# Between norm and feed-forward products: ScalarE writes the full normalised values, VectorE two low halves, three convolutions use two PSUM banks each

## The chip, the cores and the metric

The kernel runs on one core of a Trainium2 chip. The metric is the device time of one execution in microseconds, as the median of several runs. A core has TensorE (matrix products, in the profile PE, with its weight loads PEld), VectorE (DVE), ScalarE (ACT), GpSimd (POOL) and SyncE (SP, here the queue of most DMAs). Matrix products write PSUM, which has eight banks of 512 float32 columns in each of 128 partitions; GpSimd works on SBUF alone.

## What is computed

One layer of a hybrid trunk for 1024 latent tokens and 128 context tokens that share weights: a normalisation, a mixer (a gated convolution group and a gated DeltaNet group), an output projection, and then the part that matters here:

```
h  = rmsnorm(x, norm2_w) * (1 + scale2) + shift2
u, gt = split(h @ w_up)            # 2816 features each, 22 blocks of 128
gt = grid_conv3x3(gt, ffn_conv_w)  # depthwise; the context is one row
x  = x + gate2 * ((gelu(gt) * u) @ w_down)
```

Everything is float32. The kernel holds a matrix operand as a high half (rounded to the type that TensorE reads fast) and a low half (the remainder), and forms a product as high x high, low x high and high x low, three matmuls for each pair of tiles.

## The kernel before

Features lie on the partitions (8 tiles k of 128 make 1024), tokens along the columns: T = 1152, of which 1024 latent and 128 context. The five engines run programs of their own, each in the order written, and meet by semaphores; nothing is scheduled by a planner. `LATE` only gives old semaphores new names; `after(engine, what, n)` waits for one of those.

**Second norm (11 parts, list `NORM2`).** Parts 0 to 2 are the first 768 columns of tiles 0 to 2, parts 3 to 7 all columns of tiles 3 to 7, parts 8 to 10 the last 384 columns of tiles 0 to 2. For each part VectorE writes the scaled values (`scaled`, L2581) into one of two buffers `ub2`; ScalarE adds the shift and writes the high half `hH` (`high_part`, L1822); VectorE writes the low half `hL` (`low_part`, L2591); GpSimd adds both halves and writes the full value over X (`h_part`, L1607), once the old X is saved in DRAM (`x_out`). A 128-column and a 1024-column (or 256-column) instruction make up a part where latent and context differ. TensorE multiplies each part as it comes with the weights of two blocks (`norm2_step`, L3163): gate block 0 and gate block 1. Then come two more plain blocks, U_FFN+2 (the up half of block 0) and U_FFN+3 (gate block 2), 72 matmuls of 384 columns each. ScalarE copies gate block 0 into the padded grid G (`evac_rows`, L1856), gate blocks 1 and 2 into `fa` (`stage_gate`, L2056).

**Steps of seven products.** The remaining up and gate blocks are made two at a time, in 20 steps m, by a seven-product scheme (order P1, P5, P6, P3, P7, P2, P4; `FORMS`). A product is 24 matmuls of 288 columns. It needs sums of quarters of the input, made from the full values: VectorE writes four sums T1s, T3s, T2s, T4s (L2639 to L2644, 128x2304 each), ScalarE their high halves (`input_high`, L2095), GpSimd their low halves (`input_low`, L1621). It also needs sums of the weights (GpSimd, `sum_1` to `sum_4`), and of each the high half (ScalarE, `form_high`, L2090) and the low half (GpSimd, `form_low`, L1627). In a step, ScalarE copies P1, P5 and P6 out of PSUM (`copy_out`, L2114), and VectorE adds the later products: `c12` after P3, `c22_sum` after P7, `c11` after P2 (L2697, L2717), `c21` after P4 (L2725); GpSimd does `c22`. TensorE's P2 waits for `c12`, its P4 for `c22_sum`, the next step's P1 and P5 for `c11` and `c21`.

**Convolutions.** `conv9(f)` on VectorE makes block f of 22: nine taps over G on 1024 latent columns (L2664, L2667) and three on 128 context columns (L2665, L2669). The accumulator of f = 0 is the SBUF tile `fa[:, 0]`; from f = 1 it is four PSUM banks (2 to 5), 256 columns in each. The steps' combinations are written into it by hand: `beside={5: (c12, 0)}` puts `c12(0)` behind tap 5. ScalarE fills G for the next block (`gate_in`, L2066) when the convolution has ended, and applies the gelu (`gelu`, L2073 to L2076), which the next convolution waits for. `first_up` (L2685) multiplies block 0's gelu with its up half straight from PSUM.

ScalarE's order around the first step is what the change and the prediction turn on:

```
form_high(S2)
stage_gate(2, B_FFN + 3)
gate_in(1)
gelu(0)
...
        copy_out(m, p, {P1: copy_x, P5: copy_p5, P6: copy_u2}[p])
```

`gate_in(1)` waits for the end of `conv9(0)`, and the first `copy_out`, which TensorE's P6 waits for, stands behind it. P1 of step 0 is in PSUM banks 6 and 7, P5 in banks 0 and 1. SP loads the weights of a step as a pair of 512 KB tiles (`raw_pair`, L852) and stores each finished block (`p_store`, L858). After the up steps come ten down steps of the same scheme and the last norm.

Of the kernel before, what the change touches and what calls it, by code (L numbers as in the profile page):

```python
# [137 lines left out]
def build(nc, const, preds, xT, s0, wts, y_out, s_out, yc_d, g_d):  # L138
# [169 lines left out]
    def weight(k, u4):  # L308
# [5 lines left out]
        if U_FFN - 2 <= u4 < U_FFN:  # L314
# [10 lines left out]
                                for n, b in (("copy_x", 8), ("copy_p5", 9), ("copy_u2", 10)))  # L325
    sumQ = [place(f"sumQ{k}", [P, 512], F32, 229344 - 4096 + 2048 * k) for k in range(2)]
# [134 lines left out]
    def up_bank(m, p):  # L461

        first, second = (0, 3) if m % 2 else (3, 0)
        return second if p in (P5, P3, P2) else first

    def down_bank(m, p, q):

        a, b = ((1, 2), (3, 0)) if (m - UP_STEPS) % 2 == 0 else ((3, 0), (1, 2))
        return (b if p in (P5, P3, P2) else a)[q]
# [11 lines left out]
    conv_ctx = ps[:, 2, 4 * GRID:4 * GRID + CTX]  # L481

# [149 lines left out]
    with nc.Block() as block:  # L632
# [3 lines left out]
        def _(sp):  # L636
# [229 lines left out]
            for w in range(U_OUT + 2 + RAW, S0):  # L866
                after_split(N_ADA + w, w, 0)
                x_store(w - (U_OUT + 2 + RAW))
            x_store(KT - 2)
            x_store(KT - 1)  # L870
            raw_pair(0)
            raw_pair(1)
            sp.wait_ge(side_free[1], (B_FFN + 2) // 2 + 1)
            p_store(0)
            for m in range(UP_STEPS):
# [11 lines left out]
                if last:  # L887
# [3 lines left out]
                    sp.wait_ge(s["dve_step"], 8 * FB + 2)  # L891
# [648 lines left out]
        def _(pool):  # L1540
# [61 lines left out]
            def h_part(i):  # L1602

                b, cols = NORM2[i]
                pool.wait_ge(s["hL_ready"], KT + i + 1)
                lo, hi = cols[0][0], cols[-1][1]
                gp.tensor_tensor(X[:, b, lo:hi], hH[b][:, lo:hi].bitcast(F32), hL[b][:, lo:hi].bitcast(F32),  # L1607
                                 ALU.add).then_inc(s["h_ready"], 1)

            after(pool, "x_out", 16 * KT)  # L1610
            for i in range(len(NORM2)):
                h_part(i)
                if i == 4:
                    low(U_FFN + 2, U_FFN + 2)
# [52 lines left out]
            after(pool, "h_ready", len(NORM2))  # L1667
            sum_1(0)
# [52 lines left out]
        def _(act):  # L1721
# [95 lines left out]
            def high_part(i):  # L1817
# [5 lines left out]
                last.then_inc(s["hH_ready"], 1)  # L1823

# [210 lines left out]
            high_part(0)  # L2035
            square_rest(1, KT - 2, sq2[:, 0, LO:T])
# [3 lines left out]
            high_part(1)  # L2040
            log_part(1, rstd2, 1, (2,))
# [27 lines left out]
            def gelu(f):  # L2069

                act.wait_ge(s["fc_done"], f + 1)
                if not f:
                    A(fa[:, 0, :], fa[:, 0, :], ACT.Gelu_apprx_tanh).then_inc(s["gelu_done"], 1)  # L2073
                    return
# [58 lines left out]
            for m in range(UP_STEPS):  # L2133
                for p in range(FORMS):
# [4 lines left out]
                    if m == 0 and p == P1:  # L2139
                        form_high(S4)  # L2140
# [52 lines left out]
        def _(dve):  # L2193
# [451 lines left out]

            def conv9(f, beside={}):

                if f:
                    after(dve, "gt_in", f)
                else:  # L2650
                    dve.wait_ge(side_free[B_FFN % 2], B_FFN // 2 + 1)
                if f:
                    dve.wait_ge(s["gelu_done"], f)
                    if f == 1:
# [699 lines left out]
```

## Time and profile before

| | |
|---|---|
| median of 3 runs | 1531.93 us (1529.87 to 1535.61) |
| the profiled execution, its own time | 1531.26 us |
| its span, first to last instruction | 1529.4 us |
| granted TensorE clock, mean | 0.985 |
| PE busy | 1440.4 us (94%), 10534 matmuls |
| DVE busy | 1100.3 us (72%) |
| ACT busy | 597.5 us (39%) |
| POOL busy | 743.5 us (49%) |

The page also cuts the span into 40 slices of 38 us and gives TensorE's busy share in each in tenths. It is 9 in almost all of them; slices 19, 20 and 21 (688 to 803 us) show 6, 8 and 5, and slice 21 is the only one with a granted clock of 7 tenths. A timeline row is: start, duration, engine, line, operation, output<-inputs, count, and in brackets the idle time before it with what ended it. A group row gives busy time and mean duration, then the idle time before.

### The profile page before, as it was taken

What the parts mean: (1) busy time and instruction counts of PE and PEld (TensorE: products, weight loads), DVE (VectorE), ACT (ScalarE), POOL (GpSimd) and SP (SyncE); (2) the same over time, 40 slices, a digit from 0 to 9 for tenths busy, and PEclk for the clock granted to TensorE, in tenths of its full rate; (3) what the DMA queues carried; (4) which work ended last, traced back from release to release, by engine and by line L of the source; (5) the groups of instructions that cost most, each with busy time, mean ns of one, the idle gap of its engine ahead of it and who ended that gap; (6) DMA issues with size and microseconds to landing.
All of it is one profiled execution on the core that took longest, in us unless ns stands there. A gap on an engine that the chain in (4) does not pass through costs nothing. (4 is left out here: it accounts for less than half of the span.)

```text
span 1529.4 us, 26363 instructions
## 1 busy us (share of the span) xinstructions
PE 1440.4 (94%) x10534; PEld 1393.4 (91%) x10534; DVE 1100.3 (72%) x1613; ACT 597.5 (39%) x1110; POOL 743.5 (49%) x495
## 2 busy tenths in 40 slices
PE   4999999999999999996859999999999999999997
PEld 2888999999998998995859899999999989999996
DVE  4651463569996896327989766776676699999967
ACT  5322254221157785214423333333333343322324
POOL 0011111560133453223677667677666677877840
PEclk9999999999999999999979999999999999999999
DMA  9835124532416468221102121212212164333103
GB/s 336 290 138 200 62 79 130 170 114 87 144 67 191 124 194 326 88 88 36 51 16 71 66 80 71 83 63 82 76 60 87 71 240 168 107 132 134 59 29 124
DMA packets 92109, 181.04 MB, mean 118 GB/s; under 512 B 20172, under 2 KB 53524, under 8 KB 89684
## 3 DMA queue, kind: packets, MB, share of 16 engines
q1 hardware_dynamic: 88100, 169.72, 32.3%
q10 hardware_dynamic: 3456, 7.87, 1.3%
q8 instruction: 84, 1.38, 0.4%
q0 software_dynamic: 432, 1.77, 0.3%
q14 instruction: 37, 0.30, 0.1%
HBM read 140.99 MB, written 38.35 MB: 117 GB/s over the span
## 5 line engine op out<-in xcount | busy, mean ns | idle before, releaser
L2938 PE MATMUL ps<-hH,wH 128*128 128x384 f32 x696 | 237.9, 342 | 0.5 <-DVE hL L2257 0.5
L2940 PE MATMUL ps<-hL,wH 128*128 128x384 f32 x696 | 233.1, 335 | 0.0
L1627 POOL TENSOR_TENSOR wL<-sumQ,wH 128x512 fp32r<-128x512 f32 x120 | 167.5, 1398 | 121.0 <-ACT wH L2090 120.7
L2667 DVE SCALAR_TENSOR_TENSOR ps<-G,cst,ps 128x1024 f32<-128x1024 f32 x168 | 216.5, 1289 | 5.0
L1544 POOL TENSOR_TENSOR wL<-raw,wH 128x1024 fp32r<-128x1024 f32 x32 | 80.2, 2508 | 257.2 <-ACT wH L1838 256.7
L1627 POOL TENSOR_TENSOR wL<-raw,wH 128x512 fp32r<-128x512 f32 x90 | 124.0, 1381 | 76.4 <-ACT wH L2090 76.4
L2938 PE MATMUL ps<-hH,wL 128*128 128x384 f32 x696 | 158.1, 334 | 0.0
L2090 ACT ACTIVATE wH<-sumQ 128x512 fp32r<-128x512 f32 x120 | 75.6, 631 | 206.5 <-PE ps L3194 135.6
L2938 PEld LDWEIGHTS ps<-hH,wH 128*128 128x128 f32 x696 | 131.1, 188 | 8.4 <-issue 6.7
L3194 PE MATMUL ps<-hH,wH 128*128 128x288 f32 x480 | 136.0, 297 | 1.9 <-DVE fa L2697 1.9
L3197 PE MATMUL ps<-hL,wH 128*128 128x288 f32 x480 | 135.0, 295 | 0.0
L2940 PEld LDWEIGHTS ps<-hL,wH 128*128 128x128 f32 x696 | 131.1, 188 | 0.0
L2938 PEld LDWEIGHTS ps<-hH,wL 128*128 128x128 f32 x696 | 124.0, 188 | 0.0
L1838 ACT ACTIVATE wH<-raw 128x1024 fp32r<-128x1024 f32 x37 | 39.2, 1059 | 180.7 <-PE ps L2938 180.7
L3194 PE MATMUL ps<-hH,wL 128*128 128x288 f32 x480 | 103.3, 297 | 0.0
L2090 ACT ACTIVATE wH<-raw 128x512 fp32r<-128x512 f32 x90 | 56.6, 628 | 103.6 <-PE ps L3194 103.6
L3194 PEld LDWEIGHTS ps<-hH,wH 128*128 128x128 f32 x480 | 90.4, 188 | 2.2 <-issue 2.2
L3197 PEld LDWEIGHTS ps<-hL,wH 128*128 128x128 f32 x480 | 90.6, 189 | 0.0
L2801 DVE SCALAR_TENSOR_TENSOR X<-ps,mod,X 128x288 f32<-128x288 f32 (+2 forms) x240 | 81.9, 404 | 6.6 <-PE ps L3194 6.5
L3194 PEld LDWEIGHTS ps<-hH,wL 128*128 128x128 f32 x480 | 77.0, 188 | 0.0
L2291 DVE TENSOR_SCALAR acc<-zp,wqk 128x1024 f32<-128x1024 f32 (+1 forms) x24 | 21.8, 946 | 70.6 <-ACT zp L1858 70.6
L3194 PE MATMUL ps<-T2h,wH 128*128 128x288 f32 x160 | 46.6, 304 | 15.7 <-issue 15.7
(453 smaller groups left out, 4155.4 us busy)
## 6 DMA issues: line engine op xcount, KB each, us to landing
raw<-wts SPq DMA_DIRECT2D x103, 512.0 KB, 4.2
araw<-wts SPq DMA_DIRECT2D x48, 512.0 KB, 6.1
p_d<-fa SPq DMA_DIRECT2D x22, 576.0 KB
X<-xT SPq DMA_DIRECT2D x8, 1152.0 KB, 12.3
kv<-tok_d SPq DMA_DIRECT2D x16, 512.0 KB, 5.3
fs0B<-p_d SPq DMA_DIRECT2D x9, 576.0 KB, 6.6
tok_d<-stage ACTq DMA_DIRECT2D x18, 256.0 KB, 2.0
gb<-grow_d SPq DMA_DIRECT2D x18, 256.0 KB, 4.0
```

Source lines behind the costliest of these rows:

```text
L1544: nc.gpsimd.tensor_tensor(weight(1, u4), raw[:, u4 % RAW, :], weight(0, u4).bitcast(F32), ALU.subtract).then_inc(s["wl_ready"], 1)
L1627: gp.tensor_tensor(grouped(m, ring(wL, i)), form_source(m, j), grouped(m, ring(wH, i)).bitcast(F32), ALU.subtract).then_inc(s["wl_ready"], 1)
L1838: A(weight(0, u4), raw[:, u4 % RAW, :], ACT.Copy).then_inc(s["wh_ready"], 1)
L2090: A(grouped(m, ring(wH, i)), form_source(m, j), ACT.Copy).then_inc(s["wh_ready"], 1)
L2291: last = V.tensor_scalar(dst, src, w(tap), None, ALU.mult)
L2667: last = V.scalar_tensor_tensor(dst, src, w(3 * dy + dx), dst, ALU.mult, ALU.add)
L2801: last = V.scalar_tensor_tensor(X[:, ob, lo:hi], ps[:, b, at:at + hi - lo], gate(which), X[:, ob, lo:hi], ALU.mult, ALU.add)
L2938: last = M(out, lhs, rh[:, c], start=(k == 0 and not lo), stop=(lo and k == kts - 1))
L2940: M(out, lhs, rl[:, c], start=False, stop=False)
L3194: last = M(out, lhs(w, kb), rh[:, c], start=(fresh and kb == 0 and not lo), stop=(lo and kb == kbs - 1), skip_group_check=not fresh)
L3197: M(out, lhs(w, kb), rl[:, c], start=False, stop=False, skip_group_check=not fresh)
```

## The change

1. **Norm.** `h_part` on GpSimd is gone. ScalarE writes the full value of each part itself (`full_part`), right behind `high_part`, by the same instruction with X as its output. The wait for the stored X moves to ScalarE; SP waits for six stores to be complete before it issues the last two. VectorE's `scaled(i)` now also waits for `full_part(i - 2)`, since it reuses that buffer.
2. **Input sums.** The low halves of T1 and T2 move from GpSimd to VectorE, ahead of `conv9(0)`. GpSimd keeps T3 and T4, and makes them in another order among its weight sums. ScalarE makes `form_high(S1)` ahead of T1's high half, and `form_high(S4)` ahead of the loop.
3. **Early convolutions.** `conv9(0)` accumulates in banks 6 and 7, `conv9(1)` and `conv9(2)` in banks 2 and 3, 512 columns in each; their context columns stay in the SBUF tile `fa`. `conv9(3)` waits for the last combination of step 0.
4. **Banks and the first up half.** Products of step 0 use banks 4, 5 and 0, 1, the other steps swap their two pairs. So that banks 3 to 5 come free, ScalarE copies the up half of block 0 into the weight tile `raw[:, 0:2]` (`up0`), and `first_up` is one instruction that reads it there. SP loads the second pair of weights (`raw_pair(1)`) only when `first_up` is done.
5. **Combinations** of steps 0 to 2 stand at other taps.

```
+            after(sp, "x_out", 16 * (KT - 2))
             x_store(KT - 2)
             x_store(KT - 1)
             raw_pair(0)
+            sp.wait_ge(s["dve_step"], 9)
             raw_pair(1)
-            sp.wait_ge(side_free[1], (B_FFN + 2) // 2 + 1)
             p_store(0)
...
             after(pool, "h_ready", len(NORM2))
+            pool.wait_ge(s["hL_ready"], KT + len(NORM2))
             sum_1(0)
             sum_2(0)
             form_low(A11)
             form_low(S1)
-            input_low(1, 3, T1l[:], T1s[:], T1h[:])
-            input_low(2, 4, T2l[:], T2s[:], T2h[:])
-            input_low(3, 4, T3l[:], T3s[:], T3h[:])
+            sum_4(0)
+            input_low(3, 2, T3l[:], T3s[:], T3h[:])
             form_low(S2)
-            sum_4(0)
             sum_3(0)
             form_low(S4)
+            input_low(4, 4, T4l, T4s, T4h)
             form_low(S3)
-            input_low(4, 4, T4l, T4s, T4h)
...
+            def full_part(i):
+                b, cols = NORM2[i]
+                after(act, "x_out", 16 * (KT if b >= KT - 2 else KT - 2))
+                act.wait_ge(s["u_ready"], KT + i + 1)
+                for lo, hi, which in cols:
+                    last = A(X[:, b, lo:hi], ub2[:, i % 2, lo:hi], ACT.Identity, bias=mod[:, 24 + b, which:which + 1])
+                last.then_inc(s["h_ready"], 1)
...
             for i in range(2, len(NORM2)):
                 high_part(i)
+                full_part(i)
...
             form_high(A11)
+            form_high(S1)
             input_high(1, T1h[:], T1s[:])
-            form_high(S1)
             input_high(3, T2h[:], T2s[:])
             act.wait_ge(s["blk_done"], B_FFN + 3)
+            act.wait_ge(s["wl_ready"], S0)
+            for n in range(NT):
+                last = A(up0[:, n * TW:n * TW + TW], bank3((B_FFN + 2) % 2, n), ACT.Copy)
+            last.then_inc(side_free[(B_FFN + 2) % 2], 1)
             input_high(2, T3h[:], T3s[:])
             input_high(4, T4h, T4s)
+            stage_gate(2, B_FFN + 3)
             form_high(S2)
-            stage_gate(2, B_FFN + 3)
+            form_high(S4)
             gate_in(1)
             gelu(0)
...
                 if i >= 2:
                     dve.wait_ge(s["hL_ready"], KT + i - 1)
+                    after(dve, "h_ready", i - 1)
...
+            input_low(1, 3, T1l[:], T1s[:], T1h[:])
+            input_low(2, 4, T2l[:], T2s[:], T2h[:])
...
             conv9(0)
-            first_up(0)
-            conv9(1, {5: (c12, 0), 7: (c22_sum, 0)})
-            c11(0)
-            conv9(2, {2: (c21, 0)})
-            c12(1)
-            conv9(3, {2: (c22_sum, 1), 4: (c11, 1), 7: (c21, 1)})
-            conv9(4, {4: (c12, 2), 5: (c22_sum, 2), 7: (c11, 2)})
+            first_up()
+            conv9(1, {6: (c12, 0)})
+            c22_sum(0)
+            conv9(2, {1: (c11, 0), 4: (c21, 0)})
+            conv9(3, {1: (c12, 1), 4: (c22_sum, 1), 6: (c11, 1)})
+            c21(1)
+            conv9(4, {5: (c12, 2), 7: (c22_sum, 2)})
+            c11(2)
...
+                    if p == P1:
+                        if m > 1:
+                            after(pe, "out_done", 3 * (m - 1) + 2)
+                        elif m:
+                            pe.wait_ge(s["gelu_done"], 1)
+                        else:
+                            pe.wait_ge(side_free[(B_FFN + 2) % 2], (B_FFN + 2) // 2 + 1)
```

## Rows read from the trace of the kernel before

**Rows 1.** Busy by stretch: stretch, length, busy us (instructions) per engine, PEclk, DMA share, GB/s

```profile
650.00:690.00 40.00, 40.00 (x229) 39.67 (x228) 11.40 (x17) 8.57 (x10) 10.80 (x4) 1.00 0.24 84
690.00:750.00 60.00, 42.83 (x201) 38.49 (x200) 52.36 (x45) 24.23 (x39) 25.76 (x12) 0.91 0.10 38
...
780.00:800.00 20.00, 4.55 (x19) 4.58 (x20) 15.85 (x13) 6.34 (x9) 11.29 (x7) 0.58 0.07 29
...
880.00:1200.00 320.00, 320.00 (x2383) 320.00 (x2382) 213.65 (x226) 118.08 (x198) 219.93 (x170) 1.00 0.21 75
```

**Rows 2.** Groups by line and form, VectorE, 701 to 745 us

```profile
L2581 DVE SCALAR_TENSOR_TENSOR ub<-X,sc,rstd 128x1024 f32<-128x1024 f32 x5 | 17.1, 3426 | 0.1
...
L2591 DVE SCALAR_TENSOR_TENSOR hL<-ub,mod,hH 128x1024 fp32r<-128x1024 f32 x5 | 6.4, 1272 | 0.0
L2581 DVE SCALAR_TENSOR_TENSOR ub<-X,sc,rstd 128x128 f32<-128x128 f32 x8 | 4.8, 603 | 0.0
```

**Rows 3.** Groups by line and form, GpSimd, 701 to 745 us

```profile
L1607 POOL TENSOR_TENSOR X<-hH,hL 128x1152 f32<-128x1152 f32 x5 | 13.3, 2659 | 12.4 <-DVE hL L2591 12.4
...
L1544 POOL TENSOR_TENSOR wL_next<-raw,wH_next 128x1024 fp32r<-128x1024 f32 x1 | 3.3, 3347 | 0.0
```

**Rows 4.** Groups by line and form, ScalarE, 701 to 745 us

```profile
L1822 ACT ACTIVATE hH<-ub,mod 128x1024 fp32r<-128x1024 f32 x5 | 5.7, 1149 | 18.3 <-DVE ub L2581 18.3
L1822 ACT ACTIVATE hH<-ub,mod 128x128 fp32r<-128x128 f32 x8 | 3.1, 386 | 0.0
```

**Rows 5.** Timeline, TensorE, after its longest wait in the second norm

```profile
708.48 0.69 PE L3163 MATMUL ps<-hH,wH 128*128 128x384 f32 x1 [4.17 <-DVE hL L2591]
708.97 0.52 PE L3165 MATMUL ps<-hL,wH 128*128 128x384 f32 x1
```

**Rows 6.** Timeline, VectorE, first of the four input sums

```profile
745.58 2.56 DVE L2639 TENSOR_TENSOR T1s<-X 128x2304 f32<-128x2304 f32 x1 [1.12 <-POOL X L1607]
```

**Rows 7.** Groups by line and form, VectorE, 757.5 to 791.5 us: the first convolution

```profile
L2667 DVE SCALAR_TENSOR_TENSOR fa<-G,cst,fa 128x1024 f32<-128x1024 f32 x8 | 23.6, 2946 | 0.3
L2669 DVE SCALAR_TENSOR_TENSOR fa<-G,cst,fa 128x128 f32<-128x128 f32 x2 | 6.5, 3256 | 0.0
...
L2664 DVE TENSOR_SCALAR fa<-G,cst 128x1024 f32<-128x1024 f32 x1 | 1.8, 1795 | 0.0
```

**Rows 8.** Groups by line and form, GpSimd, 750 to 800 us

```profile
L1621 POOL TENSOR_TENSOR T1l<-T1s,T1h 128x2304 fp32r<-128x2304 f32 x1 | 6.2, 6156 | 0.0
...
L1621 POOL TENSOR_TENSOR T<-X,T 128x2304 fp32r<-128x2304 f32 x1 | 5.2, 5172 | 0.0
```

**Rows 9.** Timeline, ScalarE, after the first convolution

```profile
791.08 1.06 ACT L2066 ACTIVATE G<-fa 128x1024 f32<-128x1024 f32 x1 [15.88 <-DVE fa L2667]
...
792.35 1.28 ACT L2073 ACT_TABLE_LOAD   x1
793.65 1.16 ACT L2073 ACTIVATE fa<-fa 128x1152 f32<-128x1152 f32 x1
794.72 0.63 ACT L2114 ACTIVATE copy_x<-ps 128x576 f32<-128x576 f32 x1
```

**Rows 10.** Timeline, TensorE, its longest wait, and the start of the next product

```profile
795.45 0.58 PE L3194 MATMUL ps<-T2h,wH 128*128 128x288 f32 x1 [15.73 <-issue]
...
800.83 0.29 PE L3194 MATMUL ps<-hH,wH 128*128 128x288 f32 x1
```

**Rows 11.** Groups by line and form, VectorE, 860 to 1200 us

```profile
L2667 DVE SCALAR_TENSOR_TENSOR ps<-G,cst,ps 128x1024 f32<-128x1024 f32 x122 | 157.3, 1289 | 3.7
...
L2697 DVE TENSOR_TENSOR fa<-copy_x,ps 128x576 f32<-128x576 f32 x16 | 12.1, 754 | 36.9 <-PE ps L3194 36.9
...
L2669 DVE SCALAR_TENSOR_TENSOR ps<-G,cst,ps 128x128 f32<-128x128 f32 x30 | 10.5, 351 | 0.0
```

**Rows 12.** Timelines, TensorE, first and last of four waits after 816 us

```profile
817.57 0.37 PE L3194 MATMUL ps<-T1h,wH 128*128 128x288 f32 x1 [0.78 <-DVE fa L2725]
...
867.29 0.37 PE L3194 MATMUL ps<-T1h,wH 128*128 128x288 f32 x1 [1.48 <-DVE fa L2725]
```

More of the change, by code:

```diff
@@ L461, in up_bank @@
     def up_bank(m, p):
-        first, second = (0, 3) if m % 2 else (3, 0)
+        first, second = (2, 0) if not m else (3, 0) if m % 2 else (0, 3)
         return second if p in (P5, P3, P2) else first
     def down_bank(m, p, q):
-        a, b = ((1, 2), (3, 0)) if (m - UP_STEPS) % 2 == 0 else ((3, 0), (1, 2))
+        a, b = ((1, 2), (0, 3)) if (m - UP_STEPS) % 2 == 0 else ((0, 3), (1, 2))
         return (b if p in (P5, P3, P2) else a)[q]
@@ L481, in build, with early_conv @@
     conv_ctx = ps[:, 2, 4 * GRID:4 * GRID + CTX]
+    def early_conv(f):
+        k = 6 if not f else 2
+        return ps[:, k:k + 2, :]
     def units(eng, lo, hi, body):
@@ L1600, in _ @@
                 low(u, u)
[L1602 to L1614, printed above, removed]
+            low(U_FFN + 2, U_FFN + 2)
             low(U_FFN + 3, U_FFN + 3)
@@ L2035, in _ @@
             high_part(0)
+            full_part(0)
             square_rest(1, KT - 2, sq2[:, 0, LO:T])
@@ L2040, in _ @@
             high_part(1)
+            full_part(1)
             log_part(1, rstd2, 1, (2,))
@@ L2071, in gelu @@
                 act.wait_ge(s["fc_done"], f + 1)
-                if not f:
-                    A(fa[:, 0, :], fa[:, 0, :], ACT.Gelu_apprx_tanh).then_inc(s["gelu_done"], 1)
+                if f < 3:
+                    A(two(fa[:, f, 0:LAT]), early_conv(f), ACT.Gelu_apprx_tanh)
+                    A(fa[:, f, LAT:T], fa[:, f, LAT:T], ACT.Gelu_apprx_tanh).then_inc(s["gelu_done"], 1)
                     return
@@ L2644, in _, with input_low @@
             V.tensor_tensor(T4s, X[:, 4:8, 0:HT], T2s[:], ALU.subtract).then_inc(s["form_sum"], 1)
+            def input_low(n, summed, dst, src, high):
+                after(dve, "form_sum", summed)
+                after(dve, "form_high", n)
+                V.tensor_tensor(dst, src, high.bitcast(F32), ALU.subtract).then_inc(s["form_low_dve"], 1)
+            input_low(1, 3, T1l[:], T1s[:], T1h[:])
+            input_low(2, 4, T2l[:], T2s[:], T2h[:])
             def conv9(f, beside={}):
@@ L2678, in conv9, with first_up @@
                             dve.wait_ge(s["dve_step"], step)
-            def first_up(_):
+            def first_up():
                 dve.wait_ge(s["gelu_done"], 1)
-                dve.wait_ge(s["blk_done"], B_FFN + 3)
-                for n in range(NT):
-                    last = V.tensor_tensor(fa[:, 0, n * TW:n * TW + TW], fa[:, 0, n * TW:n * TW + TW],
-                                           bank3((B_FFN + 2) % 2, n), ALU.mult)
-                last.then_inc(side_free[(B_FFN + 2) % 2], 1)
+                dve.wait_ge(side_free[(B_FFN + 2) % 2], (B_FFN + 2) // 2 + 1)
+                fch.inc(V.tensor_tensor(fa[:, 0, :], fa[:, 0, :], up0, ALU.mult))
             def row_1(m, p, copy, n, lo):
@@ L3224, in _ @@
                     if not m and p in (P5, P6, P7, P4):
-                        after(pe, "form_low", {P5: 1, P6: 2, P7: 3, P4: 4}[p])
+                        after(pe, *{P5: ("form_low_dve", 1), P6: ("form_low_dve", 2), P7: ("form_low", 1), P4: ("form_low", 2)}[p])
                     product(up_bank(m, p), lambda w, kb: ring(w, i)[:, P * kb:P * kb + P], 4, up_form(p), p in (P1, P5, P2))
@@ L3234, in _ @@
                     if m % 2 == 0:
-                        after(pe, "form_low_dve", FORMS * c + p + 1)
+                        after(pe, "form_low_dve", 2 + FORMS * c + p + 1)
                     for q in range(2):
```

27 lines of the change are left out of this document (14 added, 13 removed).

## Prediction

> **What bounds the kernel now.** The table of stretches comes first [rows 1]. From 880 to 1200 us TensorE is busy in all of 320 us; there no other engine counts, and a start that is earlier by some microseconds is an end that is earlier by as much, also in the down steps, whose waits the change does not touch. What is open lies in 690 to 750 us (TensorE busy 42.8 of 60) and 780 to 800 us (4.6 of 20, clock 0.58). In the first VectorE is busy 52.4 of 60. The groups by form say with what: 1024 columns of `scaled` take 3.43 us, the same number of `low_part` 1.27, though both read two SBUF tiles [rows 2]. GpSimd's `h_part` takes 2.66 us and is released by `low_part` [rows 3], so it runs just when the next `scaled` does: 1.27 + 2.66 is near 3.4 + 0.6. The two take turns. The second place is the first convolution: its taps take 2.95 us with the accumulator in SBUF, its 128-column pieces 3.26 [rows 7], against 1.29 and 0.35 for the later ones into PSUM, which run beside a GpSimd that is just as busy (220 of 320 us) [rows 11, 1]. Once it ends, ScalarE, which waited 15.9 us for it, fills G, loads a table, applies the gelu and only then copies P1 [rows 9]; TensorE had stood for 15.7 us [rows 10].
>
> **Norm, with `h_part` gone.** A part of 1152 columns then costs VectorE 2 x (1.27 + 0.35) = 3.2 us [rows 2, 11], ScalarE 2 x (1.15 + 0.39) = 3.1 us, since the full value is one more pair of the same instructions [rows 4]. TensorE needs 18 matmuls for it in two blocks, 3.15 us at 40.0/229 = 0.175 us [rows 1]. Three engines are level. The new wait of `scaled(i)` for `full_part(i - 2)` thus costs about 0.1 us a part, and no engine queues behind it for longer. The start is a little later: the first two full values (0.9 us each) stand ahead of the squares and the logarithm of the last third on ScalarE, so that `rstd` comes some 1 us later; but `scaled(2)` and `scaled(3)` no longer wait for GpSimd, and the third part's low half, after which TensorE went on at 708.5 [rows 5], is ready at about 707.1. From there VectorE needs 5 x 3.2 + 3 x 1.4 = 20.2 us (the last three parts have a third of the columns) and waits once for GpSimd's low half of U_FFN+2, which alone is worth 2.4 (3.35 with a wait in it [rows 3]): the last full value at about 729. TensorE starts the fourth part at 710.4, waits about 3.9 us for the fifth (that low half, and ScalarE's 1.0 us for its high half), and has 10 x 1.57 + 6 x 0.52 = 18.8 us of work: done at 733.3. Before, its two plain blocks (144 x 0.175 = 25.2 us) and P1 and P5 (2 x 3.2) ended at 795.45 - 15.73 = 779.7 [rows 10], so the norm had ended at 748.1. **Gain 14.8 us.** The stores of X (SP) are unchanged but for a wait that is met; `full_part(0)` takes the wait for six of them, met before 695.
>
> **The 15.7 us wait.** P1 and P5 end at 733.3 + 31.6 = 764.9. The chain to P6: VectorE makes four sums of 2.5 us from 728.7 [rows 6], one of them behind GpSimd's low half of U_FFN+3: 741.2. T1's high half now stands behind `form_high(S1)`, which waits for GpSimd's `sum_1(0)`, queued behind that low half: 743.2, and 745.2 with its 2.05. T1 low and T2 low cost VectorE 2 x 2.5 us, not GpSimd's 6.2 each with its waits [rows 8], and wait 1.3 for its sums: 751.5. The convolution in PSUM: 9 x 1.31 + 3 x 0.35 = 12.8 us [rows 11], 764.3. G 1.3, table 1.28, gelu 1.2 and copy 0.6 [rows 9]: P6 at 768.6, a wait of 3.8 us for 15.7. **Gain 11.9 us**; together 26.7 (795.4 to 768.6).
>
> What goes against it: one piece of the first convolution was in the cheaper place. The first tap has one tile input and takes 1.79 us in SBUF among GpSimd's instructions [rows 7]; the same in PSUM takes 1.29 in the steady state. I take 1.3 us, with 0.6 and 1.8 as its ends. The Trainium skill (VectorE: DVE Perf Modes, "Why PSUM operands drop a tier") says that a float32 one-input operation runs twice as fast between SBUF tiles as with a PSUM operand. By that rule the tap would be worth 0.6 us in SBUF with GpSimd idle, and the sum 0.6 us less than for a plain exchange of 2.95 for 1.29; the trace shows no such tap alone.
>
> The 128-column pieces of the first three convolutions stay in SBUF, nine in all. With two SBUF inputs such a piece took 3.26 us [rows 7]: it waits out GpSimd's current instruction, up to the 5.2 us of T4's low half [rows 8]. Ends: 0.35 us (GpSimd idle) and 5.2. In `conv9(0)` GpSimd is mostly at weight sums or itself held up, so I take nothing there; in `conv9(1)` and `conv9(2)` 1.9 and 1.2 us. `first_up` also reads two SBUF tiles: 1.3 us, behind T4's low half until 769.3.
>
> **What is given back.** The combinations that TensorE waits for hang on the convolutions, and these are now what is late. `conv9(1)` starts at 770.6; `c12(0)` behind tap 6 comes at 770.6 + 7 x 1.31 + 3 x 0.35 + 1.9, ended at 783.3. TensorE is through P7 at 778.6: P2 waits 4.8 us. `conv9(1)` ends at 786, gelu and G 2.4, `conv9(2)` 15.3 with the two combinations in it (0.7 each), gelu and G again: `conv9(3)` starts at 806.3, `c12(1)` is done at 809.9, TensorE had been ready at 805.9: 4.1. Behind it P4 and the next P1 wait 1.8 and 0.5 for `c22_sum(1)` and `c11(1)`. In step 2 G for `conv9(4)` stands behind ScalarE's copy of P5 (828.7), `c12(2)` behind tap 5 ends at 838.4, TensorE is ready at 834.7: 3.7. Sum 15.1 us; before, four waits from 0.78 to 1.94 made 5.5 (the first and the last in [rows 12]). **Lost 9.6 us.** From step 3 on a step of TensorE's (7 x 3.22 = 22.5 us) has the 15.6 us of VectorE's inside it, as before.
>
> **Clock.** After the 15.7 us wait P6 took 5.4 us instead of 3.2 [rows 10]: 2.2 us that the kernel of before pays. After a wait of 4.2 us the clock was also at its lower level: matmuls of 0.52 us for 0.34 [rows 5]. Each such wait costs about 9 x 0.147 = 1.3 us, unless a wait follows that swallows it. The changed kernel has five waits near 4 us, two or three of them swallowed; I take 3.5 us. Ends: 0 and 6.5. **Net lost 1.3 us.**
>
> **Moved loads.** The second pair of weights is loaded after `first_up` (770.6), not after the low half of U_FFN+3. SP has `p_store(0)` behind it, which needed that instant anyhow. GpSimd's `sum_1(1)` and ScalarE's `form_high` of step 1 wait for it; landed at about 777, through six GpSimd instructions its first weights are ready near 782, and P1 of step 1 comes at 790. Nothing; if the pair took 10 us longer, 3 us. ScalarE's copy of the up half (1.2 us) is beside U_FFN+3, and P1's new wait for it is met some 10 us early.
>
> **Sum**: 14.8 + 11.9 - 9.6 - 1.3 = 15.8, and the waits of before come out 2 us too long when worked by the same steps, which I return to the give-back: 17.8 us. Against the profiled execution's 1531.26 (span 1529.4) that is 1513.5; the median is 0.7 above that execution, so 1514.
>
> **Rivals.**
> - The give-back is small (chance 0.2): ScalarE reaches its copies early enough and the clock stays up. Gain 22 to 27: 1505 to 1510. For it: before, only 5.5 us were lost there. Against: there TensorE came 27 us later on the same convolutions.
> - The give-back is large (0.2): the small pieces catch GpSimd's long instructions, each wait drops the clock. Nine pieces at 1.5 us more and 3 us of clock: gain 8 to 13, 1519 to 1524. The Trainium skill (SBUF — State Buffer, on the shared port pair) says that a VectorE operation with two SBUF inputs and a GpSimd operation exclude each other for a whole instruction, however short the one that waits; the 3.26 us of a 128-column piece agree.
> - The norm stays where it is (0.05): ScalarE's pair does not fit beside VectorE, above 5.6 us a part. Then only the second place gains, minus the give-back: within 3 us of now.
> - Slower (0.04): a tap that adds into PSUM from one SBUF tile holds off GpSimd after all when it covers two banks. Then `conv9(0)` costs 33 us as before, `conv9(1)` and `conv9(2)` 18 x (2.95 - 1.29) = 30 more, and two low halves lie on VectorE besides: P6 at 783, step 3 10 us later than before, 1540. It decides where a tap costs over about 2.4 us. Against it: 122 taps in four banks at 1.289 [rows 11].
> - The forecast itself, 1510 to 1519: 0.51.
>
> **Numbers.** The range, 1506 to 1523, takes in most of both neighbours and leaves out about 2 in 10. A measurement of this kernel can tell about 0.5% (7.7 us) from no change. Faster 0.91, within it 0.05, slower 0.04.
>
> **What would show it.** L2581 at 1.2 to 1.3 us for 1024 columns and TensorE without gaps from part 5 on; U_FFN+2 from 733; the first nine taps at 1.3; a TensorE wait ahead of P6 of 4 us; then waits of 4 to 5 us ahead of P2 in steps 0, 1 and 2, none from step 3. Wrong would be: GpSimd holding the small pieces for over 2 us each, or gaps that reach beyond step 3.

## The result and the profile after

The changed kernel takes 1513.85 us (median of 4 runs, 1505.56 to 1518.36), the kernel before beside it 1532.72 (1529.87 to 1535.61): a ratio of 0.9877, interval 0.9842 to 0.9913. The profiled execution took 1513.55 us. In a second series of 8 runs the ratio was 0.9906 (0.988 to 0.9933).

From the page of the changed kernel: its span, the busy time of TensorE and GpSimd, TensorE's slices.

```profile
span 1511.5 us, 26396 instructions
...
PE 1436.8 (95%) x10534; PEld 1391.2 (92%) x10534; DVE 1075.5 (71%) x1613; ACT 609.1 (40%) x1133; POOL 703.4 (47%) x482
...
PE   4999999999999999998979999999999989999997
```

The slices with 6, 8 and 5 are now 8, 9 and 7. By stretch (columns as in [rows 1]):

```profile
690.00:735.00 45.00, 38.53 (x197) 35.27 (x196) 35.05 (x47) 33.98 (x55) 2.39 (x1) 0.96 0.14 50
735.00:765.00 30.00, 30.00 (x180) 30.00 (x180) 23.41 (x12) 15.33 (x20) 18.62 (x8) 1.00 0.01 1
765.00:780.00 15.00, 6.87 (x41) 6.67 (x40) 10.97 (x10) 5.88 (x9) 10.44 (x6) 0.77 0.12 23
...
800.00:860.00 60.00, 52.92 (x377) 52.28 (x377) 47.05 (x48) 20.33 (x36) 34.62 (x27) 0.94 0.18 66
...
880.00:1200.00 320.00, 320.00 (x2432) 320.00 (x2432) 220.79 (x233) 121.38 (x203) 224.14 (x174) 1.00 0.21 74
```

TensorE is open in three places: inside the norm, ahead of P6 (8.1 of 15 us idle), and in the first steps. The last row holds a surprise: it is as full as before [rows 1] and yet has 2432 matmuls for 2383.

The norm, groups by form of VectorE, 704 to 735 us, which answer to [rows 2]:

```profile
L2592 DVE SCALAR_TENSOR_TENSOR ub<-X,sc,rstd 128x1024 f32<-128x1024 f32 x5 | 8.4, 1689 | 1.3 <-ACT rstd L1809 1.2
L2602 DVE SCALAR_TENSOR_TENSOR hL<-ub,mod,hH 128x1024 fp32r<-128x1024 f32 x5 | 6.4, 1279 | 0.0
```

`scaled` fell from 3.43 to 1.69 us in the mean. One of the five ran beside GpSimd's low half of U_FFN+2 and took 3.31 us; the other four took 1.28 each.

TensorE's waits behind the norm, from its timeline; all but the first answer to [rows 12], the first to [rows 10]:

```profile
776.47 0.58 PE L3216 MATMUL ps<-T2h,wH 128*128 128x288 f32 x1 [8.13 <-issue]
776.85 0.44 PE L3219 MATMUL ps<-T2l,wH 128*128 128x288 f32 x1
...
790.13 0.58 PE L3216 MATMUL ps<-hH,wH 128*128 128x288 f32 x1 [2.51 <-DVE fa L2718]
...
817.26 0.50 PE L3216 MATMUL ps<-hH,wH 128*128 128x288 f32 x1 [3.51 <-DVE fa L2718]
...
845.06 0.58 PE L3216 MATMUL ps<-hH,wH 128*128 128x288 f32 x1 [3.53 <-DVE fa L2718]
```

**Where the time went.** To compare kernels, take places of TensorE's program against one instant, VectorE's first `scaled` of the second norm. That instant itself moves by some microseconds between executions of code that is the same (694.7 and 696.4 in two of the kernel before, 697.9 and 695.3 in two of the changed one). P1, P5 and P6 stand for the start of the first matmul of that product. All in us; "step" is the time from one P5 to the next from step 4 on, the rest is everything behind the P5 of step 19.

| | P1 of step 0 | P6 | P5 of step 4 | step | rest | span | ratio to before, timed |
|---|---|---|---|---|---|---|---|
| before | 78.5 | 100.7 | 195.2 | 22.59 | 300.7 | 1529.4 | |
| before, again | 78.5 | 100.7 | 195.2 | 22.59 | 300.0 | 1530.4 | |
| changed | 64.0 | 78.6 | 180.2 | 22.12 | 301.6 | 1511.5 | 0.9877 |
| changed, again | 64.0 | 78.6 | 180.2 | 22.12 | 304.1 | 1511.4 | 0.9906 |
| norm only | 64.0 | 82.2 | 176.6 | 21.84 | 302.5 | 1502.3 | 0.9861 |
| first convolution in SBUF | 64.0 | 85.0 | 187.2 | 22.12 | 301.9 | 1521.8 | 0.9967 |
| small pieces later | 63.9 | 72.8 | 176.3 | 22.12 | 303.9 | 1507.6 | 0.9902 |
| low halves on GpSimd | 64.0 | 70.8 | 176.5 | 22.12 | 305.2 | 1509.3 | |
| other order in step 1 | 63.8 | 78.4 | 175.1 | 22.59 | 299.5 | 1508.9 | 0.9873 |
| old banks but for the first | 64.0 | 72.9 | 169.6 | 21.84 | 299.3 | 1492.2 | 0.986 |
| the same, again | 64.0 | 72.8 | 170.0 | 22.12 | 305.8 | 1502.7 | 0.9826 |
| with two repairs | 63.8 | 72.9 | 163.4 | 22.12 | 302.9 | 1498.3 | 0.9801 |

The first three columns repeat within 0.4 us in the three kernels that stand here twice. Two later runs, whose code differs from one of these only behind step 5, show that they can move by more: in one of the changed kernel P5 of step 4 came at 181.4 us, since P2 of step 2 took 5.89 us at the lower clock instead of 4.60; in one of the kernel before P1 came at 80.8, which the wait ahead of P6 took up (P6 at 100.8). So a difference of a microsecond or two between single traces is not to be read. By these columns the change gains 14.5 us up to P1, 7.6 between P1 and P6 (14.6 us for 22.2), and loses 7.1 from P6 to step 4 (101.6 for 94.5): 15.0 us. The span is 17.9 shorter: fifteen shorter steps give 7.0 more, the later start takes 3.2 and the rest 0.9. Those three also differ between executions of one kernel, as the repeats and the last experiments show.

### The profile page after: what moved, and what is told of

Same layout as the page of the kernel before. It is cut to its first block and busy times, and to the rows that moved or that the text cites. A ratio compares the mean times of both kernels' runs of the same rounds, so it can differ in the third digit from the quotient of the medians.

```text
span 1511.5 us, 26396 instructions
## 1 busy us (share of the span) xinstructions
PE 1436.8 (95%) x10534; PEld 1391.2 (92%) x10534; DVE 1075.5 (71%) x1613; ACT 609.1 (40%) x1133; POOL 703.4 (47%) x482
## 5 line engine op out<-in xcount | busy, mean ns | idle before, releaser
L2691 DVE SCALAR_TENSOR_TENSOR ps<-G,cst,ps 128x1024 f32<-128x1024 f32 x176 | 226.8, 1289 | 5.3
L2962 PEld LDWEIGHTS ps<-hL,wH 128*128 128x128 f32 x696 | 131.7, 189 | 0.0
L2301 DVE TENSOR_SCALAR acc<-zp,wqk 128x1024 f32<-128x1024 f32 (+1 forms) x24 | 21.8, 946 | 70.8 <-ACT zp L1861 70.8
L3216 PE MATMUL ps<-fh0T,wH 128*128 128x288 f32 x192 | 55.5, 303 | 6.0 <-issue 2.6
```

Of the source, the lines that this page charges most:

```text
L2301: last = V.tensor_scalar(dst, src, w(tap), None, ALU.mult)
L2691: last = V.scalar_tensor_tensor(dst, src, w(3 * dy + dx), dst, ALU.mult, ALU.add)
L2962: M(out, lhs, rl[:, c], start=False, stop=False)
L3216: last = M(out, lhs(w, kb), rh[:, c], start=(fresh and kb == 0 and not lo), stop=(lo and kb == kbs - 1), skip_group_check=not fresh)
```

## The experiments

**The repeats.** Both kernels unchanged, to see what of a profile comes again.

> The changed kernel once more, to see what repeats. Theory A: its 14.5 us in the norm and 7.6 us ahead of P6 repeat, but the step of seven products in the steady state (22.12 us in its first trace, 22.59 before) is a state of the execution and not of the kernel: in some traces of either kernel it is 22.1, in others 22.6. Rival: the shorter step belongs to the changed kernel (22.12 again here, 22.6 in every kernel with the banks of before).

> The kernel before once more, for its trace. So far the steady step of seven products took 22.59 us in its one trace, 22.12 in four traces of kernels with the changed loop and 21.84 in the one with the norm's part alone, and each product's time in a trace stays the same from one wait of TensorE to the next. Theory A (the step's length is fixed by where TensorE's last wait falls, so by the kernel): 22.59 again, and every time up to the fifth step within 0.3 us of the first trace. Rival (it differs from execution to execution): 22.12 or 21.84 here.

Second and fourth line of the table; median of the changed kernel 1513.44 us (8 runs, 1508.14 to 1519.5). The waits came again within 0.2 us. So did the steps, 22.12 and 22.59 us, which fits a length that the kernel sets; the last experiment speaks against that.

**The norm alone.** The kernel before with `full_part`, the new wait of `scaled` and the stores of part 1, nothing else.

```
-            for i in range(len(NORM2)):
-                h_part(i)
...
             for i in range(2, len(NORM2)):
                 high_part(i)
+                full_part(i)
```

> The kernel before with the norm's part of the change alone (full values by ScalarE). Theory A: the norm ends 14.5 us earlier after its first scaled tile, the wait ahead of P6 stays near 15.7 us, and the whole gain reaches the end: about 14 to 15 us less than before. Rival: the early convolutions take turns with GpSimd in another way once the norm is shorter, and half of it is lost in front of P6 (7 us less).

Median 1505.62 us, ratio 0.9861 (0.9814 to 0.9909). P1 comes at the same 64.0 us: the norm's 14.5 us are part 1 and nothing else. But P5 of step 4 comes 18.6 us earlier than before, 4.0 of them ahead of P6, which was not expected; the whole change gains 15.0 there. **Parts 2 to 5 lose 3.6 us between them**, by one trace of this kernel and two of the changed one; the intervals of the timed ratios overlap. The wait ahead of P6 is 11.73 us, shorter than before (15.73) and longer than in the changed kernel. The later ones are at the places of before, 0.55 to 1.95 us each:

```profile
777.77 0.58 PE L3197 MATMUL ps<-T2h,wH 128*128 128x288 f32 x1 [11.73 <-issue]
...
799.90 0.37 PE L3197 MATMUL ps<-T1h,wH 128*128 128x288 f32 x1 [1.59 <-DVE fa L2728]
```

Its first convolution is in SBUF and takes turns with GpSimd, yet starts 13.4 us earlier after the same instant (42.4 for 55.8). In the changed kernel the low halves of T1 and T2 stand ahead of it, and VectorE waits 6.37 us for T1's high half before it can make them.

**The first convolution back in SBUF**, all else as changed.

```
+                if not f:
+                    dst, dctx, rows = fa[:, 0, 0:LAT].rearrange("p (r c) -> p r c", c=GRID), fa[:, 0, LAT:T], lambda ap: ap
```

> The changed kernel with the first convolution's accumulator back in the SBUF tile. Theory A (two SBUF inputs and a GpSimd instruction take turns): its taps take above 2 us instead of 1.29 while GpSimd works, the convolution some 8 to 13 us longer, and TensorE waits 16 to 20 us ahead of P6 instead of 8.1; 8 to 12 us slower than the changed kernel. Rival (the gain at P6 came from the low halves moved to VectorE and the shorter queue of GpSimd): taps near 1.3 to 1.5 us, under 3 us slower.

Median 1522.82 us, ratio 0.9967 (0.9933 to 1.0001). P6 comes 6.4 us later (a wait of 14.53), step 4 7.0: slower, as the theory had it, but by less than its 8 to 12. The groups by form of VectorE, 756.5 to 785 us:

```profile
L2693 DVE SCALAR_TENSOR_TENSOR fa<-G,cst,fa 128x1024 f32<-128x1024 f32 x8 | 16.0, 1999 | 0.3
L2690 DVE TENSOR_SCALAR fa<-G,cst 128x1024 f32<-128x1024 f32 x1 | 5.7, 5657 | 0.0
```

A tap costs 2.00 us here in the mean, where it was 2.95 [rows 7]; GpSimd is busy for 15.9 of these 28.5 us, and was for 29.7 of 34 in the kernel before. Even the first tap, with a single tile as input, waited: 5.66 us.

**The small pieces.** The changed kernel's own wait ahead of P6 was 8.13 us for a forecast of 3.8. VectorE's timeline of its first convolution:

```profile
753.66 1.27 DVE L2688 TENSOR_SCALAR ps<-G,cst 128x1024 f32<-128x1024 f32 x1
754.85 4.01 DVE L2689 TENSOR_SCALAR fa<-G,cst 128x128 f32<-128x128 f32 x1
758.90 5.27 DVE L2691 SCALAR_TENSOR_TENSOR ps<-G,cst,ps 128x1024 f32<-128x1024 f32 x4
764.07 1.26 DVE L2693 SCALAR_TENSOR_TENSOR fa<-G,cst,fa 128x128 f32<-128x128 f32 x1
765.37 1.29 DVE L2691 SCALAR_TENSOR_TENSOR ps<-G,cst,ps 128x1024 f32<-128x1024 f32 x1
766.56 1.47 DVE L2693 SCALAR_TENSOR_TENSOR fa<-G,cst,fa 128x128 f32<-128x128 f32 x1
```

and GpSimd's beside it:

```profile
752.99 5.79 POOL L1616 TENSOR_TENSOR T3l<-T3s,T3h 128x2304 fp32r<-128x2304 f32 x1 [1.67 <-ACT T3h L2102]
763.90 1.29 POOL L1622 TENSOR_TENSOR wL<-sumQ,wH 128x512 fp32r<-128x512 f32 x1 [5.12 <-ACT wH L2097]
...
766.60 1.28 POOL L1622 TENSOR_TENSOR wL<-sumQ,wH 128x512 fp32r<-128x512 f32 x1
```

The first piece ends at 758.86, T3's low half at 758.78; the second at 765.33, GpSimd's at 765.19; the third at 768.03 and 767.88. Each ended with what GpSimd was at. Two have two SBUF inputs, the first, dearest one has a single tile as input. The Trainium skill (SBUF — State Buffer, "Who interferes with whom") counts such one-input operations among those that can take the shared pair; the 4.01 us agree. The taps around them, which write to PSUM, stayed at 1.3.

In this kernel the same three pieces stand behind taps 4, 5 and 6, instead of 0, 4 and 5:

```
+                pieces = {4: 0, 5: 1, 6: 2} if not f else {0: 0, 4: 1, 5: 2}
```

> The changed kernel with the three 128-column pieces of the first convolution behind taps 4, 5 and 6 instead of 0, 4 and 5. Theory A (they wait out GpSimd's instruction, the first one T3's low half for 3.7 us): the first piece takes 0.35 us, the convolution is 3 to 5 us shorter, the wait ahead of P6 4 us instead of 8.1, and the waits ahead of P2 in steps 0 to 2 move with VectorE, so that 3 to 4 us reach the end. Rival: TensorE's later waits are set by ScalarE and by TensorE's own clock, and P6 earlier by 4 us only lengthens the wait ahead of P2: under 1 us at the end.

Median 1511.53 us, ratio 0.9902 (0.9868 to 0.9935). VectorE's timeline:

```profile
757.87 0.28 DVE L2694 TENSOR_SCALAR fa<-G,cst 128x128 f32<-128x128 f32 x1
...
759.39 0.35 DVE L2696 SCALAR_TENSOR_TENSOR fa<-G,cst,fa 128x128 f32<-128x128 f32 x1
...
760.97 0.35 DVE L2696 SCALAR_TENSOR_TENSOR fa<-G,cst,fa 128x128 f32<-128x128 f32 x1
...
767.83 4.02 DVE L2711 TENSOR_TENSOR fa<-fa,raw 128x1152 f32<-128x1152 f32 x1 [3.86 <-ACT fa L2080]
```

P6 comes 5.8 us earlier, just what the pieces had held (4.01 + 1.26 + 1.47 is 5.8 above three free ones, 0.28 + 0.35 + 0.35). Of that 3.9 are left at step 4: `first_up`, with two SBUF inputs, now meets T4's low half (4.02 us, for 1.36 in the changed kernel), and P2 waits 7.12 us for `c12(0)`. The wait ahead of P2 of step 1 falls to 0.91 us, with a new one of 1.35 ahead of P4; the one of step 2 stays at 3.53.

**The two low halves** back on GpSimd, behind `form_low(S1)`.

```
-            input_low(1, 3, T1l[:], T1s[:], T1h[:])
-            input_low(2, 4, T2l[:], T2s[:], T2h[:])
...
+            for n, summed, dst, src, high in ((1, 3, T1l, T1s, T1h), (2, 4, T2l, T2s, T2h)):
...
+                gp.tensor_tensor(dst[:], src[:], high[:].bitcast(F32), ALU.subtract).then_inc(s["form_low_dve"], 1)
```

> The changed kernel with the low halves of T1 and T2 back on GpSimd. Theory A (GpSimd's queue and the wait of the small pieces behind its long instructions): two more 5.1 us instructions stand in front of its weight sums, and T3's low half; VectorE starts the first convolution about 7 us earlier but each of its three SBUF pieces waits up to 5 us; P6 comes 0 to 4 us earlier or later than the changed kernel's 78.6 us after the norm's first tile. Rival (P5 itself has to wait for T1's low half): TensorE gets a new wait ahead of P5 and P6 is over 4 us later.

One run, 1511.34 us. The convolution starts 13.4 us earlier (7 were expected), P6 comes at 70.8 for 78.6 (0 to 4 us were expected), and step 4 comes 3.7 us earlier. Its pieces still wait (1.23, 5.18 and 3.96 us), and so does the first one of `conv9(1)` (4.01). TensorE now waits twice for GpSimd, for little, and for `c12(0)` 3.9 us longer than in the changed kernel:

```profile
766.57 0.37 PE L3217 MATMUL ps<-T2h,wH 128*128 128x288 f32 x1 [0.32 <-POOL wL L1622]
...
773.94 0.40 PE L3217 MATMUL ps<-T3h,wH 128*128 128x288 f32 x1 [0.81 <-POOL wL L1622]
...
783.77 0.58 PE L3217 MATMUL ps<-hH,wH 128*128 128x288 f32 x1 [6.40 <-DVE fa L2719]
```

**The combinations.** In step 1 of the changed kernel P2 waits for `c12(1)`, which stands behind tap 1 of `conv9(3)`, and that starts only when G is filled; in step 2 VectorE stands 7.08 us for G, which ScalarE fills behind its copy of P5. This kernel puts `c12(1)` ahead of `conv9(3)` as before, and lets ScalarE apply gelu 3 and fill G behind P1:

```
-            GELU = {0: {P7: 1}, 1: {P6: 2}, 2: {P5: 3, P2: 4}}
+            GELU = {0: {P7: 1}, 1: {P6: 2}, 2: {P1: 3, P2: 4}}
...
-            conv9(3, {1: (c12, 1), 4: (c22_sum, 1), 6: (c11, 1)})
+            c12(1)
+            conv9(3, {0: (c22_sum, 1), 4: (c11, 1)})
```

> The changed kernel with c12(1) ahead of the fourth convolution, c22_sum(1) and c11(1) at its taps 0 and 4, and ScalarE's third gelu and fifth filling of G behind P1 instead of P5 of step 2. Theory A (what is given back is the order of the combinations and of ScalarE's queue): the waits ahead of P2 in steps 1 and 2, 3.5 us each with 1.6 us of lower clock behind each, shrink to under 1 us; the fourth step starts 5 to 9 us earlier than in the changed kernel. Rival (VectorE's chain of convolutions is full): at most 2 us.

Median 1508.82 us, ratio 0.9873 (0.983 to 0.9916). The waits ahead of P2 in steps 1 and 2 are gone. Two others have come in their place, 1.82 us ahead of P1 of step 2, for `c11(1)`, and 2.67 ahead of its P5. Step 4 comes 5.1 us earlier, at the lower end of what was expected, but the span is only 2.6 shorter: all later steps took 22.59 us, not 22.12.

**The old banks.** The changed norm, sums and first up half, but only `conv9(0)` accumulates in two banks, 4 and 5, with its context columns in bank 3; the other convolutions have four banks, and the combinations and the steps' banks are those of before.

```
+    first_acc, first_ctx = ps[:, 4:6, :], ps[:, 3, 0:CTX]
...
-        first, second = (2, 0) if not m else (3, 0) if m % 2 else (0, 3)
+        first, second = (0, 3) if m % 2 else (3, 0)
```

> The changed kernel with the first convolution in banks 4 and 5 and its 128 context columns in bank 3, all freed by ScalarE's copy of the up half; all later convolutions, products and combinations use the banks, taps and order of the kernel before. Theory A (the small pieces in SBUF and the new order of combinations are what costs): the first convolution takes 12.8 to 13.5 us instead of 18.3, P6 comes near 73 us after the norm's first tile instead of 78.6, the second to fifth convolution follow each other as before (51.8 us instead of 58.4), and the fourth step starts 8 to 12 us earlier than in the changed kernel, 5 to 8 earlier than with the norm's part alone. Rival (ScalarE, which blocks on a gelu while TensorE is ahead, holds the copies): P2 of step 0 and P6 of step 1 wait, and it is level with the norm's part alone.

Median 1501.08 us, ratio 0.986 (0.9801 to 0.9919). No piece of `conv9(0)` waits now (18.3 us become 12.7), and step 4 comes 10.6 us earlier than in the changed kernel, 7.0 earlier than with the norm alone. Three of the six waits of TensorE are

```profile
768.56 0.37 PE L3208 MATMUL ps<-T2h,wH 128*128 128x288 f32 x1 [2.38 <-issue]
...
781.40 0.58 PE L3208 MATMUL ps<-hH,wH 128*128 128x288 f32 x1 [2.93 <-DVE fa L2711]
...
793.03 0.38 PE L3208 MATMUL ps<-T1h,wH 128*128 128x288 f32 x1 [0.51 <-DVE fa L2739]
```

From the start of `conv9(1)` to that of `conv9(4)` it takes 51.8 us, as the kernel of before does; the changed one takes 58.4. This run changes the small pieces, the banks and the places of the combinations together. In the changed kernel the six small pieces of `conv9(1)` and `conv9(2)` hold 4.7 us more than free ones would, so they can be most of the 6.6; the rest was not taken apart.

**The best version** adds two repairs: GpSimd makes T4's low half behind `form_low(A22)`, where it no longer meets `first_up`, and gelu 3 and G stand behind P1 as above.

```
-            input_low(4, 4, T4l, T4s, T4h)
             form_low(S3)
             form_low(A12)
             form_low(A22)
+            input_low(4, 4, T4l, T4s, T4h)
```

> The kernel with the first convolution in banks 4, 5 and 3, and in addition T4's low half behind the three weight halves S3, A12 and A22 on GpSimd, and ScalarE's third gelu and fifth filling of G behind P1 of step 2. Theory A (VectorE's chain from the first convolution to the fifth sets the start of the third step): first_up takes 1.4 us instead of 4.05, the second convolution starts 2.7 us earlier, the fifth 3 us more; the fourth step starts 4 to 6 us earlier than there (169.6 us after the norm's first tile). What becomes of the end depends on the length that the steps settle on: 21.84 would give a span near 1487, 22.59 one near 1499. Rival (P4 has to wait for T4's low half, or ScalarE for P1): under 1 us.

Median 1499.07 us, ratio 0.9801 (0.9753 to 0.985): the lowest of all, though its interval meets those of the old banks and of the norm alone. `first_up` takes 1.36 us, and the waits of TensorE are down to 2.52, 0.23, 1.72, 1.04 and 0.63 us, the 0.23 being that ahead of P2 of step 0. Step 4 comes 6.2 us earlier than with the old banks alone (4 to 6 were expected), 16.8 earlier than in the changed kernel, 31.8 earlier than before.

**The length of a step.** From step 4 to step 18 TensorE never waits and its granted clock is 1.00 in every kernel of the table, yet a step takes 21.84, 22.12 or 22.59 us. The idea was that each wait of TensorE sets the length for all that follows until the next one. So both kernels got one harmless wait for work in P1 of step 6:

```
+                    if p == P1 and m == 6:
+                        after(pe, "out_done", 3 * (m - 1) + 3)
```

> The changed kernel with one more wait of TensorE: P1 of step 6 also waits for c21 of step 5, which it would have waited for at P5. Cost of the wait itself 1 to 2 us. Theory (a product's length is drawn anew at each restart of TensorE and then kept): the steps up to the sixth take 22.12 us as before, those behind it another of the three lengths seen, 21.84 or 22.59, or 22.12 by chance. Rival (the length belongs to the kernel's addresses or to the chip): 22.12 on both sides.

> The kernel before with the same extra wait ahead of step 6. Theory (drawn anew at a restart): up to step 5 22.59 us, behind it a length that may be shorter; at 21.84 the thirteen steps left would give back 9.8 us for a wait of 1 to 2, so that a kernel with one wait more is up to 8 us faster; at 22.12 it gains 4 to 5. Rival: 22.59 on both sides and 1 to 2 us slower.

In the changed kernel (one run, 1522.93 us) the wait was 1.37 us, at 918 us, and the stretches on either side of it are

```profile
880.00:915.00 35.00, 35.00 (x268) 35.00 (x267) 22.05 (x24) 13.10 (x23) 25.26 (x20) 1.00 0.23 78
925.00:1200.00 275.00, 275.00 (x2047) 275.00 (x2047) 184.81 (x194) 102.53 (x172) 189.13 (x147) 1.00 0.20 73
```

that is 131 and 134 ns a matmul: the steps went from 22.12 to 22.59 us. In the kernel before it was 1.30 us, at 934 us:

```profile
880.00:930.00 50.00, 50.00 (x374) 50.00 (x373) 31.91 (x34) 18.04 (x30) 33.83 (x27) 1.00 0.23 81
940.00:1200.00 260.00, 260.00 (x1977) 260.00 (x1976) 175.50 (x187) 99.21 (x166) 182.81 (x142) 1.00 0.21 75
```

134 and 132 ns: from 22.59 to 22.12. The length changes at one wait, in either direction, and then stays. The first steps show the same: in the best version a product took 3.23 us behind the wait of 1.72, 3.12 behind that of 1.04 and 3.16 behind that of 0.63. As a tool the wait is worth nothing: timed, the kernel before with the wait has a ratio of 1.0011 (0.9984 to 1.0037), median of 10 runs 1529.18 us. Last, the version with the old banks ran again, unchanged, since its first profile had shown 21.84:

> The same kernel as e8_banks, run again, to see whether the length of its steady step belongs to the kernel or to the execution. Theory 'kernel': the last TensorE wait of the early steps falls at the same place and sets the length, so the step is 21.84 us again (320 us from 880 us on hold 2464 matmuls) and the profiled execution takes 1492 to 1497 us. Rival 'execution': the length is drawn in each execution; the step is 22.12 or 22.59 us as likely as 21.84 (2432 or 2383 matmuls), and the execution takes 4 to 11 us more. The early part is the same by both: P5 of step 4 at 169.6 us, within 0.5, after VectorE's first scaled tile of the second norm. The median of the timed runs near 1501 us by both, 1495 us if the profiled length were that of all executions.

Median 1503.72 us, ratio 0.9826 (0.9794 to 0.9857). First its row of the first time, then of the second:

```profile
880.00:1200.00 320.00, 320.00 (x2464) 320.00 (x2463) 224.30 (x237) 122.85 (x206) 227.80 (x177) 1.00 0.22 79
```

```profile
880.00:1200.00 320.00, 320.00 (x2433) 320.00 (x2432) 220.45 (x232) 121.05 (x202) 224.69 (x175) 1.00 0.21 76
```

Up to step 4 the two executions agree within 0.4 us; then a step took 22.12 for 21.84 us and the rest 305.8 for 299.3. **The kernel alone does not set the length.** The two ran on different chips, but the chip alone does not set it either, since it changed within one execution in both runs above. The two traces of the kernel before differ too, where the step length of both is 22.59: behind P6 of step 0 a product took 3.16 us in one and 3.12 in the other. That the kernel before settled on 22.59 in each of its three traces and the changed one on 22.12 leaves open whether some kernels favour one length. The timed medians agree with lengths that change from execution to execution. What they gain on before (1528 times one minus the ratio: 21.2 norm only, 5.0 the first convolution in SBUF, 21.4 and 26.6 the old banks, 19.4 the other order, 30.4 the best, 15.0 small pieces later, 14.4 and 18.8 the changed kernel) stays within 4.3 us of the gain at step 4 (18.6, 8.0, 25.6 and 25.3, 20.1, 31.8, 18.9, 15.0), while each interval is 4 to 9 us wide to either side; with the profiled step lengths added, "norm only" would be 29.8 and the old banks 36.8, which their intervals leave out.

## Why the prediction was right, and where it was not

It said 1514 us; measured were 1513.85. The sign and the size stand, the steps behind them less so, and that the two numbers meet within 0.2 us is luck.

- **Norm: right.** 14.8 forecast, 14.5 measured, and the norm-only kernel shows the same without the rest. `scaled` costs 1.28 us beside an idle GpSimd, and TensorE has no gap from part 5 on (one of 3.22 us ahead of it, for 3.9).
- **The wait ahead of P6: the step that failed.** Forecast 3.8 us, measured 8.13; the gain there was 7.6, not 11.9. The prediction "took nothing" for the 128-column pieces of `conv9(0)`, on the ground that GpSimd is mostly at weight sums or held up. They cost 5.8 us above free ones, and moving them by a few taps gave that back. The rows were at hand: such a piece had taken 3.26 us in the mean in the first convolution of before [rows 7], and low halves of 5.2 to 6.2 us stayed on GpSimd [rows 8]; here it was T3's that the first piece met. The range of such a piece had been put at 0.35 to 5.2 us; the end at which it was taken was wrong. The sum ahead of it held: the convolution starts 55.8 us after the instant, for a forecast of 56.8 (751.5 less 694.7), though the two low halves took 3.46 and 3.66 us, not 2.5.
- **The give-back: right in kind.** Waits ahead of P2 in steps 0, 1 and 2 and none from step 3, as forecast, but 2.51, 3.51 and 3.53 us for 4.8, 4.1 and 3.7, and none of the 1.8 and 0.5 at other products; with those the forecast waits make 14.9 us, not the 15.1 of the text. VectorE's side of them:

```profile
777.14 1.28 DVE L2688 TENSOR_SCALAR ps<-G,cst 128x1024 f32<-128x1024 f32 x1
...
789.23 0.75 DVE L2718 TENSOR_TENSOR fa<-copy_u,ps 128x576 f32<-128x576 f32 x1
...
835.58 1.29 DVE L2688 TENSOR_SCALAR ps<-G,cst 128x1024 f32<-128x1024 f32 x1 [7.08 <-ACT G L2073]
```

  The first wait is short for two reasons: `conv9(1)` starts 0.7 us behind P6 and not 2.0, since `first_up` found T4's low half done, and TensorE took 11.15 us for P6, P3 and P7, not 10.0, since P6 ran at a lower clock.

  *The clock.* Behind each of the four waits the granted clock was 0.64 to 0.67 in 4.7 to 4.8 us (the lower of its two levels for most of it, matmuls of 0.44 us for 0.29), and the product took 4.6 to 4.8 us for 3.16, some 1.6 each. From `conv9(1)` to P2 of step 1 VectorE's idle times end with ScalarE's filling of G, which itself waited for VectorE; so the 1.6 us of P6 and of P2 of step 0 went into the next wait, as the prediction allowed for. The other two reach step 4: `conv9(4)` starts 6.8 to 6.9 us behind P5 of step 2 in six traces, and no wait stands behind P2 of step 2. That is 3.2 us, near the 3.5 that the prediction took. The 2.2 us that it set against them for the kernel before were no cost there: P6 took 5.38 us in it and 4.57 in the norm-only kernel, and P5 of step 1 came 22.1 us behind P6 in both, so the wait ahead of it took them up. Net the clock cost 3.2 us, not 1.3.

  *The total.* That the sum of before came out 2 us too long, which the prediction returned, stands there without its working; no run shows that term, and P6 to step 4 took 94.5 us before and 101.6 after. Lost 7.1 us, against 8.9 forecast (9.6 and 1.3 less the 2.0 returned).
- **The sum.** 14.5 + 7.6 - 7.1 = 15.0 us for a forecast 17.8. That the profiled execution came out at -17.9 is 7.0 us of shorter steps, which the prediction took for equal, against 4.1 of start and rest. These vary between executions of one kernel. The medians of the two series, 18.9 and 15.3 us below before, cannot tell 15.0 from 17.8.
- **The rivals.** "The give-back is large" had the right mechanism, pieces that catch GpSimd's long instructions. They held 5.8 us ahead of P6, where the forecast had nothing, and 4.7 in the next two convolutions, where it had 3.1. The rival's price does not follow from its terms: nine pieces at 1.5 us and 3 us of clock take 16.5 from the 17.8, which leaves 1.3 and not 8 to 13. The slower case did not come: a tap into two banks takes 1.29 us beside GpSimd, as one into four.
- **Not seen at all:** that parts 2 to 5 are worth less than nothing beside part 1. The prediction priced them against the kernel before, whose first convolution ran beside GpSimd's many instructions, and not against one in which the norm alone had moved. There the parts gain 3.6 us ahead of P6 (78.6 for 82.2) and lose 7.2 behind it. At step 4 the two low halves on VectorE cost 3.7 us (one trace) and the first convolution in PSUM is worth 7.0. What loses the rest lies between `conv9(1)` and `conv9(4)`, 58.4 for 51.8 us: the small pieces of two convolutions in SBUF (0.5 to 1.4 us each) and the new places of the combinations, which no run here takes apart.

## What to carry to other kernels

A short VectorE instruction between SBUF tiles cost here what was left of GpSimd's current instruction, so place it against GpSimd's timeline, or move its accumulator to PSUM; three such pieces cost 5.8 us, more than four taps of 1024 columns. Price each part of a change beside the other parts, not beside the kernel before: here one part alone was at least as good as all five, and that part with a few of the others reached step 4 7.0 and 13.2 us before that one part alone. Compare kernels by places in the program counted from a common instant, and only then by the span, since the steady stretch moves by itself. A cost that is followed by a wait for another engine may not count: look for what sets the end of that wait.

## What the runs showed of the hardware

The clock at 1.00 does not fix the length of a steady stretch. The same 168 matmuls of 288 columns in a step took 21.84, 22.12 or 22.59 us, 130.0, 131.7 or 134.5 ns each, constant to a hundredth of a microsecond from step to step, changed at a single wait of 1.3 or 1.4 us, and different in two executions of one kernel. Over fifteen steps that is 11.2 us, more than most parts of this change. The Trainium skill (TensorE: Matmul & The Clock Gate, "Back-to-back issue gap") gives columns over 2.4 GHz and 2.5 ns for a matmul by itself, which is an estimate of 122.5 ns for 288 columns; all three lengths lie above it. Why there are just these three, and what a wait changes, stays open; no run here reached it. The rest behind P5 of step 19 takes between 299.3 and 305.8 us, 6.5 us apart in two executions of one kernel. Of these, 5.0 are waits of TensorE of over 0.2 us in step 19 and the down steps: 10 of together 9.4 us in the faster execution, 22 of 14.4 in the slower one, most of them for VectorE's additions, and the second down step took 21.84 us in the one and 26.85 in the other. Why they come in one execution and not in the other stays open.

A wait of TensorE does not always cost clock behind it. Ahead of P2 of step 2 the wait was 1.95 us in the kernel before and in the norm-only kernel alike; behind it the granted clock was 1.00 in the one, and the product took 3.21 us, and 0.64 in the other, where it took 4.82.
